# A hybrid decoder step on one core: the first prompt tile goes ahead of the other tiles at the end of phase one

## What is computed

```python
h = rms_norm(x, norm1_w);  z = h @ w_in            # q | k | v | conv GLU | gates
A = silu(layer_norm(depthwise_conv31(glu(z)))) @ w_conv_proj
B = dilated_attention(q, k, v) @ w_attn_proj       # 3 groups x 8 heads
x1 = x + (sig(gA) * A + sig(gB) * B) @ w_out
h2 = rms_norm(x1, norm2_w)
q = h2 @ w_peer_q                                  # 8 heads x 2 halves x 128
s = q . sub_keys                                   # 128 scores each half
idx, g = top16(top16(s[0]) + top16(s[1]))          # 16 experts of 128^2 each head
y = x1 + sum_k g_k * gelu(h2 . expert_u[idx_k]) * expert_v[idx_k]
```

## Time and profile before

| | before |
|---|---|
| three runs, us | 2147.18, 2151.61, 2158.86 (median 2151.61) |
| the profiled execution, its own time, us | 2151.05 |
| span of its trace, us | 2149.1 |
| PE, DVE, ACT, POOL busy | 74%, 64%, 38%, 37% of the span |
| bytes moved | 745.14 MB, of them 570.46 MB by POOL's queue |
| granted TensorE clock, mean | 0.83 of full speed |

### The profile page before, as it was taken

One profiled execution on the slowest core, in us unless ns is written; L12 is line 12 of the kernel. 1 busy time (PEld: TensorE's weight loads), 2 busy tenths in 40 slices (PEclk: granted clock), 3 DMA queues, 4 the chain that ended last, 5 costly groups with the idle time before them and its releaser, 6 DMA issues.

```text
span 2149.1 us, 33388 instructions
## 1 busy us (share of the span) xinstructions
PE 1597.1 (74%) x11692; PEld 729.1 (34%) x11692; DVE 1374.1 (64%) x3347; ACT 825.1 (38%) x2404; POOL 793.7 (37%) x713
## 2 busy tenths in 40 slices
PE   7989999898998997777778988895444445444444
PEld 3556655444444443434433433341100001110000
DVE  1477655123468788967766666447767767777774
ACT  2133333201545535544546533334433333433332
POOL 1255100001323354444532322344555554455553
PEclk9999999999999999999989999997555556655555
DMA  5433466837999999999999999999999999999998
GB/s 186 150 115 115 174 221 237 312 138 246 384 414 386 385 372 422 375 364 385 360 393 378 389 417 410 401 418 394 421 421 421 419 413 403 416 418 416 421 412 345
DMA packets 125794, 745.14 MB, mean 347 GB/s; under 512 B 15892, under 2 KB 39052, under 8 KB 47916
## 3 DMA queue, kind: packets, MB, share of 16 engines
q0 software_dynamic: 78336, 570.46, 65.6%
q1 hardware_dynamic: 47292, 172.55, 21.5%
HBM read 727.36 MB, written 16.44 MB: 346 GB/s over the span
## 4 chain that ended last, share of the span: by engine, by line
PE 36%; DMA 26%; DVE 20%; issue 7%; ACT 4%; POOL 2%; SPq 0%; DVEq 0%; POOLq 0%; ACTq 0%; PEldq 0%
DMA ring<-in_expert_uv,pick 24%; PE z L1210 20%; DVE ring L1990 7%; PE acc L1382 5%; PE z L1216 1%; PE s L1235 1%; DVE ti L1873 1%; ACT fold L1555 1%; DMA ring<-in_v_cache 1%; DVE ti L1876 1%; POOL ring L1139 1%; DVE tv L1875 1%; PE o L1245 1%; PE s L1512 1%; ACT gel L1552 1%
## 5 line engine op out<-in xcount | busy, mean ns | idle before, releaser
L1139 POOL DMA_INDIRECT ring<-in_expert_uv,pick x544 | 662.1, 1217 | 874.5 <-PE acc L1382 806.2
L1990 DVE CUSTOM_DVE_ANT_0 ring<-ring,rep 128x1024 f32<-128x1024 f32 x544 | 664.8, 1226 | 405.0 <-DMA ring<-in_expert_uv,pick 356.9
L1382 PE MATMUL acc<-ring,fold 128*32 128x256 f32 x4352 | 455.1, 505 | 451.5 <-ACT fold L1555 451.0
L1210 PE MATMUL z<-wts,hT 128*128 128x384 f32 (+1 forms) x1408 | 599.8, 563 | 4.1 <-DMA wts<-in_w_glu 2.4
L1382 PEld LDWEIGHTS acc<-ring,fold 128*32 128x32 f32 x4352 | 104.0, 124 | 774.7 <-ACT fold L1555 712.7
L1210 PEld LDWEIGHTS z<-wts,hT 128*128 128x128 f32 x1408 | 255.4, 195 | 251.0 <-issue 181.0
L1552 ACT ACTIVATE gel<-dots 128x1 f32<-128x1 f32 x544 | 108.6, 200 | 594.6 <-DVE dots L1990 593.4
L1210 PE MATMUL z<-wts,yT 128*128 128x512 f32 x384 | 184.4, 615 | 3.0 <-ACT yT L1570 1.6
L1555 ACT ACTIVATE fold<-by_pick,gel 128x32 f32<-128x32 f32 x544 | 174.8, 321 | 18.1
L1548 ACT ACTIVATE by_pick<-cst,pick 128x32 f32<-128x32 f32 x544 | 167.3, 308 | 0.0
L1865 DVE SCALAR_TENSOR_TENSOR yT<-uT,vec,yT 128x256 f32<-128x256 f32 x240 | 106.0, 496 | 2.0
(11 more groups left out here) (291 smaller groups left out, 1688.6 us busy)
## 6 DMA issues: line engine op xcount, KB each, us to landing
wts<-in_w_qkv SPq DMA_DIRECT2D x24, 1536.0 KB, 8.1
wts<-in_w_glu SPq DMA_DIRECT2D x8, 2048.0 KB, 12.7
wts<-in_w_gate SPq DMA_DIRECT2D x8, 2048.0 KB, 11.9
wts<-in_w_wq SPq DMA_DIRECT2D x8, 2048.0 KB, 11.6
ring<-in_k_cache SPq DMA_DIRECT2D x16, 768.0 KB, 7.9
ring<-in_v_cache SPq DMA_DIRECT2D x16, 768.0 KB, 7.4
ring<-in_expert_uv,pick POOLq DMA_INDIRECT x544, 11.3
wts<-in_w_cp SPq DMA_DIRECT2D x4, 2048.0 KB, 11.7
```

The lines of the kernel that those rows point to most:

```text
L1139: eng.indirect_dma_start(ring[:, i % RING, :], None, a["expert_uv"], bass.IndirectOffsetOnAxis(picks(i, 0).bitcast(U32), 0)).then_inc(row_ ...
L1210: mm = eng.matmul(bank[:, 0:w], of[:, k, :], rows[:, k, :], start=(k == 0), stop=(k == depth - 1))
L1382: mm = eng.matmul(acc[b][SUB * c:SUB * (c + 1), col:col + 256], fold[:, i % 4, :], ring[:, i % RING, D + 256 * c:D + 256 * (c + 1)], start ...
L1990: eng.tensor_tensor_reduce(u, u, rep[:, j, :], 1.0, 0.0, ALU.mult, ALU.add, dots[:, i % 4:i % 4 + 1]).then_inc(dot_ready, 1)
```

## The change

`plan()` no longer puts the blocks `cp` 1 to `wq` 1 of phase one to use for all tiles in turn. A list written by hand gives the order: tile 0 runs `cp` 1, `ap` 0, `ap` 1, `wo` 0, `wo` 1 and `wq` 0, with tiles 1 and NT filling in between. That needs more than two blocks at once, so `ap` 0 lies in ring slot 3, `ap` 1 in slot 4, and the two halves of `wo` 1 in slots 2 and 5, each when the samples' attention is through with the slot. The other blocks keep the two slots of `wts` by turns. Gathers into slots 2 to 5 wait for the last product with the block that lies there. `START` moves from tick 242 to 231; the cap of 16 steps stays. The second half of the samples' first value product (`DV` 0, 1) and of the second (`DV` 1, 1), with their `DE` and `DH`, stand two ticks later. Work and transferred bytes stay the same.

```diff
@@ plan @@
+    after = {"cp": behind_cp, "ap": behind_ap, "wo": behind_wo, "wq": behind_wq}
...
-                         (18, ("DV", 0, 1)), (19, ("DE", 0)), (21, ("DH", 0))):
+                         (20, ("DV", 0, 1)), (21, ("DE", 0)), (23, ("DH", 0))):
...
-        for half in range(2):
+        for half in range(2 if p else 1):
             for t, e in each(p, "cp", half):
-                put(e + 1, ("c", t, half))
+                behind_cp(t, half, e)
+        late = []
+        if p == 0:
+            units += [("cp", 0, 1), ("ap", 0, 0), ("ap", 0, 1), ("wo", 0, 0), ("wo", 0, 1), ("wq", 0, 0), ("wq", 0, 1)]
+            late = [("cp", 0, 1), ("ap", 0, 0), ("ap", 0, 1), ("cp", 1, 1), ("cp", NT, 1), ("wo", 0, 0), ("wo", 0, 1), ("ap", 1, 0), ("ap", 1, 1), ("ap", NT, 0), ("ap", NT, 1),
+                    ("wq", 0, 0), ("wo", 1, 0), ("wo", NT, 0), ("wo", 1, 1), ("wo", NT, 1), ("wq", 0, 1), ("wq", 1, 0), ("wq", NT, 0), ("wq", 1, 1), ("wq", NT, 1)]
+        for kind, t, j in late:
...
+            if (kind, t, j) == ("wq", 0, 0):
+                now = max(now, ends["wo", 0, 1] + 6)
+            e = use(t, kind, j)
+            after[kind](t, j, e)
@@ homes of the weight blocks @@
+IN_RING = {UNIT_NO["ap", 0, 0]: (3,), UNIT_NO["ap", 0, 1]: (4,), UNIT_NO["wo", 0, 1]: (2, 5)}
...
+def weight_homes():
+    last, count = [None, None], [0, 0]
+    for u in range(len(UNITS)):
+        if u not in IN_RING:
+            s = sum(count) % 2
+            WTS_SLOT[u], WTS_BEFORE[u], WTS_LOAD[u] = s, last[s], count[s]
+            last[s], count[s] = u, count[s] + 1
@@ SP, load @@
+                if u in IN_RING:
+                    eng.wait_ge(tp_ready, TB.no["DT", 1, 1] + 1)
+                elif WTS_BEFORE[u] is not None:
+                    eng.wait_ge(z_ready, last_use(WTS_BEFORE[u]) + 1)
...
+                for x, r in enumerate(IN_RING[u]):
+                    if r < 3:
+                        eng.wait_ge(k_used, 8)
+                    elif r == 5:
+                        eng.wait_ge(tp_ready, TB.no["DH", 1] + 1)
+                        eng.wait_ge(d_out, 16 * HP * NG)
+                    eng.dma_start(ring[:, r, :], a["w_" + kind][n][:, 2 * D * x:2 * D * (x + 1)]).then_inc(w_ring_in[u], 16)
@@ POOL, gathers @@
+                    if i in RING_NEEDS:
+                        eng.wait_ge(z_ready, RING_NEEDS[i])
@@ PE, products with a block @@
-                rows = buffer(unit_of(u)).rearrange("p (k c) -> p k c", k=depth)
+                rows = weight_rows(unit_of(u), depth)
```

More of the change, by code:

```diff
@@ L249, in inputs, with behind_cp, behind_ap, behind_wo @@
         put(at + 3, ("XT", t, 1))
+    def behind_cp(t, half, e):
+        put(e + 1, ("c", t, half))
+    def behind_ap(t, half, e):
+        put(e + 1, ("a", t, half))
+        put(e + 2, ("MT", t, half))
+    def behind_wo(t, j, e):
+        put(e + 1, ("w", t, j))
+        if j == 0:
+            return
+        put(e + 2, ("N0", t))
+        s = 2 if t == NT else 0
+        if t == NT:
+            put(e + 3, ("ND", t))
+            put(e + 4, ("NP", t))
+        put(e + 3 + s, ("N1", t))
+        put(e + 4 + s, ("ro", t))
+        put(e + 4 + s, ("HT", t, 0))
+        put(e + 5 + s, ("HT", t, 1))
+    def behind_wq(t, j, e):
+        put(e + 1, ("k", t, j))
+        put(e + 2, ("QT", t, j))
+        put(e + 4, ("SC", t, j))
+        put(e + 5, ("so", t, j))
+    after = {"cp": behind_cp, "ap": behind_ap, "wo": behind_wo, "wq": behind_wq}
     for p in range(2):
@@ L327, in plan @@
                 put(first + d, (name, NT))
-            again = max(first + 23, conv_last + 6)
+            again = max(first + 25, conv_last + 6)
             for d, v in ((0, ("DS", 1, 0)), (5, ("DS", 1, 1)), (6, ("DN", 1)), (7, ("DM", 1)), (8, ("DT", 1, 0)), (9, ("DT", 1, 1)), (13, ("DV", 1, 0)),
-                         (18, ("DV", 1, 1)), (19, ("DE", 1)), (21, ("DH", 1))):
+                         (20, ("DV", 1, 1)), (21, ("DE", 1)), (23, ("DH", 1))):
                 put(again + d, v)
@@ L338, in plan @@
+        for kind, t, j in late:
+            if kind == "rest":
+                now += 1
+                continue
+            if (kind, t, j) == ("wq", 0, 0):
+                now = max(now, ends["wo", 0, 1] + 6)
+            e = use(t, kind, j)
+            after[kind](t, j, e)
+        if p == 0:
+            inputs(2, now)
+        for half in range(2 if p else 0):
             for t, e in each(p, "ap", half):
-                put(e + 1, ("a", t, half))
-                put(e + 2, ("MT", t, half))
+                after["ap"](t, half, e)
@@ L341, in plan @@
         assert p or again + 21 < ends["ap", NT, 0]
[L342 to L356, removed]
@@ L357, in plan @@
-        now = ends["wo", PAIRS[p][0], 1] + 6
-        for j in range(4):
-            for t, e in each(p, "wq", j):
[L360 to L365, removed]
+        if p:
+            now += 1
+            for j in range(2):
+                for t, e in each(p, "wo", j):
+                    after["wo"](t, j, e)
+            now = ends["wo", PAIRS[p][0], 1] + 6
@@ L366, in plan @@
+        for j in range(0 if p else 2, 4):
+            for t, e in each(p, "wq", j):
+                after["wq"](t, j, e)
+            if p == 0 and j == 2:
+                inputs(3, now)
         ends["conv", p] = (conv_first, conv_last)
@@ L402, in last_use, with tick_of @@
     return USE_NO[(s[0], PAIRS[s[1]][-1], *s[2:])]
+def tick_of(task):
+    return next(n for n, some in enumerate(TICKS) if task in some)
+RING_FROM = {u: tick_of(("DT", 1, 1)) if max(rs) < 5 and min(rs) > 2 else tick_of(("DH", 1)) if max(rs) == 5 else tick_of(("DV", 1, 1)) for u, rs in IN_RING.items()}
+RING_NEEDS = {r: max(USE_NO[(UNITS[u][0], NT, *UNITS[u][2:])] + 1 for u, rs in IN_RING.items() if r in rs) for r in sorted({r for rs in IN_RING.values() for r in rs})}
 def tick_phase(n):
@@ L773, in program @@
         lng, lnb = vec[:, :, TAPS + 2], vec[:, :, TAPS + 3]
-        w_in = sems("w_in", 2)
+        w_in, w_ring_in = sems("w_in", 2), {u: sem(f"w_ring_in{r}") for u, (r, *_) in IN_RING.items()}
         rest_in = sem("rest_in")
@@ L964, in _ @@
             for n, tick in enumerate(TICKS):
-                while loaded < len(UNITS) and ENDS[USES[last_use(loaded - 2)]] < n:
+                while loaded < len(UNITS) and (RING_FROM[loaded] if loaded in IN_RING else ENDS[USES[last_use(WTS_BEFORE[loaded])]]) < n:
                     load(loaded)
```

27 lines of the change are left out of this document (18 added, 9 removed).

## The result

The changed kernel takes 2160.4 us (median of 9 runs, 2155.5 to 2167.8) against 2153.8 (9 runs) of the kernel before, a ratio of 1.0034 with a 95% interval of 1.0017 to 1.0050. Forecast were 2156.3 us and "within 0.5%": it is that, but on the slow side. The profiled execution took 2157.7 us with a span of 2155.9, against 2151.05 and 2149.1. Phase two starts at 604.42 us (597.33 before), 7.1 us later, and from there to the end it is 1551.5 us (1551.8 before). So the whole loss lies ahead of phase two, and nothing comes back behind it.

A forecast was written before the change was run, and what follows sets the result against it. Transfers were taken to set the pace behind the first gather, PE the start of phase two. Terms -1.2 + 3.3 + 1.4 + 3.5 + 1.7 = +8.7, less 4.0, gave +4.7 and 2156.3 us; range 2143 to 2168.

The forecast's parts named there:

- `DV` 0, 1: Samples' first value product, second half: standing two ticks later removes its 1.23 us wait for values, -1.2 us.
- `DV` 1, 1: Samples' second value product, second half: weight blocks queued ahead delay its values; wait grows from 3.85 to 7.1, +3.3 us.
- First search: PE at the first search: waits of 3.5 for `w` and 2.7 for picks instead of one of 4.76, +1.4 us.
- POOL and `ND`: Small norm product `ND`: gathers ahead of the power on POOL make PE wait, +3.5 us.
- First step: PE's wait of 1.96 us for the first expert step stays, 0 (from -3.8 to +2).
- The clock: PE's granted clock ahead of phase two: one more fall behind waits, +1.7 us (0 to 6.8).
- rival 3: Clock falls at every wait from `DV` 1, 1 to the first step: +13.8 us, 2165.5; chance 0.19.
- The start of phase two: Sum of PE's waits and clock in phase one: phase two starts 8.7 us later, near 606.
- rival 4: Change does not do what it says, for one a late `wq` 2 block: +2 to +5; 0.55 together with the forecast.
- The lead, -4.0: Start of phase two: 1.6 MB of gathers already moved saves 4.0 us of transfers (0 if PE can't use it).
- Rival 2: Lead is kept: the transfer-bound stretch starts 18 us earlier and so does the end, 2134; chance 0.08.
- Rival 1: Waits at values and POOL do not come, clock falls no further, the 1.6 MB is gained: -7.7 us, 2144; chance 0.18.

The follow-up runs named there:

- e1: Changed kernel with block `wo` 0 requested one tick later, behind the fourth value piece instead of ahead of it: 2153.8 us, ratio 1.0003 to the kernel before.
- e6: Changed kernel with tile 1's first `w` ahead of the first search on DVE and PE's pick-spreading product `P` four ticks later: 2164.0 us, ratio 1.0048.
- e5: Changed kernel with POOL issuing two gathers, then the power of tile 1's norm, then the other four gathers: 2156.5 us, ratio 1.0012 to the kernel before.
- e3: Changed kernel with the cap of steps in phase one raised from 16 to 32 (29 reached): 2151.5 us, ratio 0.9993 to the kernel before.
- e4: Changed kernel with eight zero products on PE ahead of the wait for the fourth value piece: 2160.6 us in one run.
- e2: Changed kernel meant to hold four of 22 gathers until phase two; they started only 14 to 19 us later, still ahead of it: 2162.0 us, ratio 1.0034.
- e9: Changed kernel with the fourth value piece requested ahead of `wo` 0 and POOL's power ahead of four gathers: 2150.1 us, ratio 0.9977 to the kernel before.
- e10: Changed kernel with value piece ahead of `wo` 0, POOL's power ahead of four gathers, and cap raised to 32 (29 steps reached): 2140.8 us, ratio 0.9938.
- e12: Kernel before, with cap 32 and one step per 2.0 us of PE's products (30 steps in phase one): 2169.9 us, ratio 1.0074 to the kernel before.

## Why the prediction was right, and where not

The forecast was a time within 0.5% of before, and it is; the time is 4.1 us above the forecast, inside the range. Step by step:

- **`DV` 0, 1** two ticks later, -1.2: its wait is gone. By the second block of key scores (376 us) the changed kernel is 2.6 us ahead, of which 1.2 stood there before any changed work. Right. The key scores' slow stretch did not come in this execution, which is counted with the clock.
- **`DV` 1, 1**, a wait of 7.1: 6.75. PE came at 425.6, not 430.1, since it was 4 us ahead, and the piece was there by 432.3 instead of 437.2. Both ends were off by 4.5 to 4.9 us, and the difference held. e1 shows that the mechanism is the queue.
- **First search**, 3.5 + 2.7: 3.63 + 0.94. The second is smaller because the 12 instructions between took 6.87 us at the lower clock instead of 5.3 and hid part of it. e6 shows a coupling that the prediction did not have: it counted this place and POOL's as two prices, while both hang on when `P` is done.
- **POOL and `ND`**, 3.5: 2.60, since four gathers took 4.65 us from 507.75 on, not 5.8; PE came 22.8 us behind `SC`, where 22.7 were expected. e5 shows the mechanism.
- **First step**, 0: 1.96 before and 1.96 after, and so in every kernel above.
- **The clock**, one more fall at 1.7: four falls where two were. The term was mis-sized, about +3.1 instead of +1.7: from the second key scores to phase two PE is busy 203.7 us for 1520 instructions, and 200.6 for the same 1520 before. Named one by one, the slow products give 2.35 + 1.45 + 1.57 + 1.6, about 7.0 us in the changed kernel and 3.4 in the kernel before, where one of the two falls was at the key scores. That is rival 3's picture at half its price: five waits above 1.9 us and four slow stretches, but the one at 390 with none.
- The start of phase two, **+8.7**: +7.1. The rows give -2.6 + 2.9 - 0.2 + 2.6 + 3.1 = +5.8; the other 1.3 us are short waits, put at 0 (PE is idle 24.4 us in that stretch instead of 17.7, 5.3 of them named here). None of them is a wait for a weight block, so the doubt about covers and rival 4 did not come.
- **The lead, -4.0**: -0.3, and this is the step that failed. "All that the lead can still deliver at that point is 1.6 MB" took it that transfers set the pace from there. The page's slices, which are at nine tenths from the 11th slice on and not from the 16th, say so only on the average. In the first 200 us of phase two PE walks the same list with the same 11.6 us of waits for folds, and its steps up to 53 stay as far behind as phase two does. The 0 that the prediction had beside its 4.0, "if PE can't use it", was the right value. The rests of single profiles differ by as much as 4 us (see the last section), so it is these steps that show it, and not the -0.3.

With the lead at nothing the forecast would have been 2160.3, and 2160.4 was measured. Part of that is luck: the clock was missed by 1.4 us one way and the waits by 3.0 the other (4.0 for 7.0, short ones counted), and the median of the kernel before is 2153.8 over nine runs where three had shown 2151.6. As a difference, the sum without the lead asks for 8.7 us, and 6.6 were measured.

The idle transfer time that the prediction saw in the last ticks of phase one is there as well, for 12 of the 20 us from 590 to 610.

Rival 2 (the lead is kept) gave 2134, and the result refutes it: the first gather is 19.7 us earlier and the end is later. e3 shows what the cap of 16 steps kept from it: 26 us behind phase two's start for 14.6 ahead of it. Rival 1 fell at e1, whose queue it denied, and at e5.

The Trainium skill (TensorE: Matmul & The Clock Gate, HAM oscillation) says that work behind an idle gap of the array starts at half clock. Weighed again: behind waits of 6.6 us and more the rows show it each time, and in the one profile of e4 filling the gap removes it; behind the 2.2 to 2.4 us ahead of the key scores it came in 3 of 14 profiles (2.80 us for 48 instructions without, 4.10 to 4.48 with). The Trainium skill ties the fall to the gap; here one and the same gap has it in one execution and not in another.

## What to carry to other kernels

Ask which list paces at the place where a lead arrives. Here 1.5 gathers more brought nothing to an engine that walked its own list, while 13 steps finished early took their products and waits out of it. Before an experiment is read, look in its trace whether the edit did what it was for: in e2 it did not. When a block is requested earlier, look at what is behind it in the same queue and due first: one request moved by a tick was worth the whole loss. A reordering's gain can be locked behind an old limit such as a cap; here the order lost 0.34% with the limit and gained 0.62% without it and with two queues put right.

## What the runs showed of the hardware

- A wait's length does not fix what the clock does behind it. Behind the same 3.63 us the same 12 instructions took 6.87 us in the changed kernel, 7.08 in e1 and e9, 8.40 in e5, 8.41 in e4 and 8.46 in e10. The granted clock from 490 to 500 is 0.83 of full speed in the changed kernel and 0.69 in e5: parts of the stretch are at 1.2 GHz and the rest at 2.4, in shares that differ from one execution to the next.
- Behind 3.85 us the kernel before had no slow stretch, and the same products behind 4.05 us in e12 took 5.34 us instead of 3.64. Waits of 2.60 us at `ND` had slow products behind them in the changed kernel (2.99 us for 4 instructions) and none in e4 (1.88 behind 2.61).
- The profiled executions' rests vary by some 4 us for the same number of early steps (1550.0 to 1554.1 in nine kernels with 16), so a difference of that size between two profiles says nothing.
